# Embedding gate of a two-block transformer kernel: first weight slab tile by tile, the second tile's transposes between, embedding copies moved in ScalarE's queue

## What is computed

```python
h = h + FFN_RES_WEIGHT * swiglu(rms_norm(h, ffn2_norm[i]), ffn2_w_in[i], ffn2_w_out[i])
ple_gate = jax.nn.sigmoid(rms_norm(h, ple_norm[i]) @ w_ple_gate[i])
h = h + ple_gate * (p[i] @ w_ple_proj[i])
```

## Time and profile before

| | us |
|---|---|
| median of 3 runs | 1374.62 (1373.52 to 1375.25) |
| profiled execution | 1375.29 |
| its span, first to last instruction | 1373.5 |
| mean granted TensorE clock | 0.981 of full speed |

### The profile page before, as it was taken

The page is one execution under the profiler, slowest core; times in us unless marked ns, Lnnn a source line. Parts: engine busy times, 40 slices in busy tenths (PEclk is TensorE's granted clock), DMA queues, the critical chain, the costliest instruction groups (busy, mean ns, idle before and its releaser), DMA issues.

```text
span 1373.5 us, 23083 instructions
## 1 busy us (share of the span) xinstructions
PE 1330.2 (97%) x9022; PEld 1212.8 (88%) x9022; DVE 942.6 (69%) x1369; ACT 766.1 (56%) x1150; POOL 203.3 (15%) x165
## 2 busy tenths in 40 slices
PE   9999999999999999999999999989999999999997
PEld 8999989888998999989998889989998777777775
DVE  6555575486566555566688775765765799999996
ACT  5333346565545333355554677325734677777774
POOL 1222220030001222220301322410001000202020
PEclk9999999999999999999999999989998999999999
DMA  9655544522345555534443344215455599999991
GB/s 315 212 185 188 185 143 155 187 93 93 131 153 175 191 185 186 178 127 154 162 159 127 123 139 136 93 62 181 138 172 184 205 403 363 342 368 335 372 330 43
DMA packets 73943, 263.44 MB, mean 192 GB/s; under 512 B 8320, under 2 KB 9600, under 8 KB 73728
## 3 DMA queue, kind: packets, MB, share of 16 engines
q1 hardware_dynamic: 72864, 260.39, 55.2%
q10 hardware_dynamic: 992, 1.86, 0.4%
HBM read 261.17 MB, written 1.05 MB: 191 GB/s over the span
## 4 chain that ended last, share of the span: by engine, by line
PE 70%; DVE 9%; ACT 4%; issue 2%; POOL 0%; DVEq 0%; ACTq 0%
PE bank L561 21%; PE bank L563 20%; PE bank L562 20%; DVE sb_wlo L518 3%; DVE sb_wlo L505 2%; PE bank L2792 1%; ACT sb_aw L1729 1%; PE bank L2771 1%; ACT sb_Uh L636 1%; DVE sb_XC L2119 1%; PE bank L653 1%; PE bank L741 1%; PE bank L2849 1%; ACT sb_XC L1700 1%; ACT sb_whi L513 0%
## 5 line engine op out<-in xcount | busy, mean ns | idle before, releaser
L505 DVE TENSOR_TENSOR sb_wlo<-sb_raw,sb_whi 128x1024 fp32r<-128x1024 f32 (+2 forms) x304 | 383.4, 1306 | 168.5 <-ACT sb_whi L489 168.3
L489 ACT ACTIVATE sb_whi<-sb_raw 128x1024 fp32r<-128x1024 f32 (+3 forms) x308 | 302.0, 1031 | 227.9 <-PE bank L563 222.3
L561 PE MATMUL bank<-sb_Uh,sb_whi 128*128 128x256 f32 x1216 | 349.9, 288 | 9.7 <-ACT sb_sgh L1693 4.0
L562 PE MATMUL bank<-sb_Ul,sb_whi 128*128 128x256 f32 x1216 | 346.1, 285 | 0.0
L563 PE MATMUL bank<-sb_Uh,sb_wlo 128*128 128x256 f32 x1216 | 346.0, 285 | 0.0
L561 PEld LDWEIGHTS bank<-sb_Uh,sb_whi 128*128 128x128 f32 x1216 | 235.2, 193 | 14.9 <-issue 9.4
L562 PEld LDWEIGHTS bank<-sb_Ul,sb_whi 128*128 128x128 f32 x1216 | 235.4, 194 | 1.1 <-issue 0.2
L563 PEld LDWEIGHTS bank<-sb_Uh,sb_wlo 128*128 128x128 f32 x1216 | 235.3, 194 | 0.0
L561 PE MATMUL bank<-sb_whi,sb_Uh 128*128 128x256 f32 (+3 forms) x560 | 162.3, 290 | 6.7 <-DVE sb_Ul L645 4.9
L562 PE MATMUL bank<-sb_wlo,sb_Uh 128*128 128x256 f32 (+3 forms) x560 | 160.1, 286 | 0.0
L563 PE MATMUL bank<-sb_whi,sb_Ul 128*128 128x256 f32 (+3 forms) x560 | 159.9, 286 | 0.0
(11 more groups left out here) (407 smaller groups left out, 2252.3 us busy)
## 6 DMA issues: line engine op xcount, KB each, us to landing
sb_raw<-in_slabs SPq DMA_DIRECT2D x162, 512.0 KB, 4.5
sb_raw<-in_ffn_in SPq DMA_DIRECT2D x88, 512.0 KB, 4.6
sb_raw<-in_moe_in SPq DMA_DIRECT2D x50, 512.0 KB, 5.6
sb_raw<-in_ffn_out SPq DMA_DIRECT2D x44, 512.0 KB, 3.9
sb_raw<-in_moe_out SPq DMA_DIRECT2D x26, 512.0 KB, 6.0
sb_deep_free<-in_moe_in SPq DMA_DIRECT2D x16, 512.0 KB, 5.7
sb_deep_uh<-in_moe_in SPq DMA_DIRECT2D x16, 512.0 KB, 5.2
sb_deep_ul<-in_moe_in SPq DMA_DIRECT2D x16, 512.0 KB, 6.0
```

The costliest lines, as they stand in the source:

```text
L489: nc.scalar.activation(whi[:, i % NSLOT, c], raw[:, i % NSLOT, c], ACT.Copy).then_inc(S("hi_done"), 1)
L505: nc.vector.tensor_tensor(wlo[:, i % NSLOT, c], raw[:, i % NSLOT, c], whi[:, i % NSLOT, c].bitcast(F32), ALU.subtract).then_inc(S("lo_done ...
L561: pe.matmul(o, lh, rh, start=start, stop=False, skip_group_check=True)
L562: pe.matmul(o, lh, rl, start=False, stop=False, skip_group_check=True)
```

## The change

In `tokens_by_pairs` the first slab can now be done tile by tile: tile 0 for all eight chunks, then a given piece of work, then tile 1. For the embedding gate that piece is the turn of tile 1, which PE did before the slab until now. The other two calls of the function stay as they were. In ACT's queue the embedding copies move behind the chunks of tile 1.

```diff
-        def tokens_by_pairs(names, banks, done, made, tile_done, in_last):
+        def tokens_by_pairs(names, banks, done, made, tile_done, in_last, next_tile=None):
...
                 if j == 0:
-                    wh, wl = wslab(s0, KD, 256)
-                    for k in range(KD):
-                        if k in (0, KD // 2):
-                            pe.wait_ge(*reach("lo_done", 2 * s0 + (2 if k else 1)))
-                        for t in range(NT):
-                            stage, base, step = made(t)
-                            pe.wait_ge(*reach(stage, base + k // step + 1))
-                            last = mm3(bank[b[t]][:, 0:256], Uh[:, k, tile_cols(t)], Ul[:, k, tile_cols(t)], wh[:, k], wl[:, k],
-                                       k == 0, k == KD - 1)
+                    if next_tile is not None:
+                        token_tile(s0, b[0], 0, Uh, Ul, KD, 256, made=made(0))
+                        next_tile()
+                        last = token_tile(s0, b[1], 1, Uh, Ul, KD, 256, made=made(1))
+                    else:
...
             act_turned("n4", 0, "ple_norm")
+            act_turned("n4", 1, "ple_norm")
             ple_proj_out(1)
-            act_turned("n4", 1, "ple_norm")
...
             ple_proj(1)
-            for t in range(NT):
-                pe_turn("n4", t)
+            pe_turn("n4", 0)
             tokens_by_pairs([f"pgate{c}" for c in range(4)], pg_bank, "pg", lambda t: ("n4_lo", KD * t, 1), "t_x4",
-                            (6, lambda: pe_turn("n5", 0)))
+                            (6, lambda: pe_turn("n5", 0)), next_tile=lambda: pe_turn("n4", 1))
```

More of the change, by code:

```diff
@@ L678, in tokens_by_pairs @@
                 if j == 0:
-                    wh, wl = wslab(s0, KD, 256)
-                    for k in range(KD):
-                        if k in (0, KD // 2):
-                            pe.wait_ge(*reach("lo_done", 2 * s0 + (2 if k else 1)))
-                        for t in range(NT):
-                            stage, base, step = made(t)
-                            pe.wait_ge(*reach(stage, base + k // step + 1))
-                            last = mm3(bank[b[t]][:, 0:256], Uh[:, k, tile_cols(t)], Ul[:, k, tile_cols(t)], wh[:, k], wl[:, k],
-                                       k == 0, k == KD - 1)
+                    if next_tile is not None:
[3 more added lines that the diff above has]
+                    else:
+                        wh, wl = wslab(s0, KD, 256)
+                        for k in range(KD):
+                            if k in (0, KD // 2):
+                                pe.wait_ge(*reach("lo_done", 2 * s0 + (2 if k else 1)))
+                            for t in range(NT):
+                                stage, base, step = made(t)
+                                pe.wait_ge(*reach(stage, base + k // step + 1))
+                                last = mm3(bank[b[t]][:, 0:256], Uh[:, k, tile_cols(t)], Ul[:, k, tile_cols(t)], wh[:, k], wl[:, k],
+                                           k == 0, k == KD - 1)
                     last.then_inc(S("slab_used"), 1)
```

## The result

| | before | after |
|---|---|---|
| median of 20 runs, us | 1373.47 | 1375.48 |
| lowest to highest | 1370.63 to 1375.25 | 1370.15 to 1377.82 |
| profiled execution, span | 1375.29, 1373.5 | 1373.34, 1371.5 |

The ratio after to before is 1.0017, with a 95% interval of 1.0009 to 1.0025: slower by 2.3 us, 1.2 to 3.4. The ratio itself is inside the 0.2% that was called no change; the interval ends above it.

What follows compares the result with a forecast made beforehand. PE, busy 97% of the span, bounds the kernel, so time is won only where it stands still or runs at low clock. -0.53 + 1.46 = +0.93 us on the 1374.62 median gives 1375.55, stated as 1375.5; range 1373.0 to 1377.4.

Steps and rivals of the forecast that it cites:

- Tile 0 and the second turn: In pgate0, PE keeps up with tile 0's corrections, then turns tile 1 at 613.08; ACT idles 1.54 us.
- T1: Time at which PE finishes tile 0 of pgate0 and tile 1's transposes start, put at 613.08 us.
- ACT's way to the split: On ACT, tile 1's chunks (3.24 us) and copies (0.96) precede pgate1's split, at 617.92, 1.53 us later than before.
- The stall: PE waits 2.34 us for pgate1's first half, about 2.2 as counted; pgate1 starts 0.53 us sooner than before.
- The clock: PE's clock falls to 1.2 GHz behind the new idle before pgate1, costing 1.46 us; bounds 0 and +1.46.
- case B: Stall moved to before pgate1, clock stays at 2.4 GHz: -0.53 us, 1374.1; chance 0.28.
- case A: The forecast: stall moved to before pgate1, clock falls, +0.93 us, range 1374.6 to 1376.5; chance 0.58.
- The sum: Whole kernel: -0.53 us at pgate1's start plus 1.46 for the low clock gives +0.93 us.
- C: Gain comes whole, pgate1's first half ready by 617.96: -2.87 us, 1371.75; chance 0.05.
- D: The chunk-paced part of pgate0 itself runs at the low clock: +2.7 us, 1377.35 or above; chance 0.09.

Runs made afterwards that it cites:

- after_2: The changed kernel timed again with no edit; 1.0016 (1.0004 to 1.0029) of the kernel before.
- before_fill: The kernel before with 14 matmuls on zeros added on PE behind the two turns; 0.9996 of the kernel before.
- early_half: The changed kernel with pgate1's first half split between the two tiles' chunks, second half behind tile 1, then copies; 0.9985 and 0.9987 of the kernel before.
- copies_only: The kernel before with only the embedding copies moved behind tile 1's chunks in ACT's queue, PE's order kept; 0.9990 of the kernel before.

## Why the prediction came out

The forecast was 1375.5 and the median after is 1375.48. That it is so close is luck, two errors that cancel: the 1374.62 it started from was the median of three runs and stood at 1373.47 after twenty, and against +0.93 us the runs show +2.3, 1.2 to 3.4. The direction was right, the new stall and its cause came out as worked out, and so did the price of a fall; the size of the whole was too small.

- **Tile 0 and the second turn.** T1 was put 613.08 - 608.20 = 4.88 us behind the first turn; it is 611.18 - 606.30 = 4.88. ACT's idle of 1.54 us: 1.54.
- **ACT's way to the split.** Forecast 9.72 us behind the first turn, measured 10.00. Tile 1's chunks took 615.34 - 611.82 = 3.52 us up to the copies, not 3.24: there is one wait of 0.35 us ahead of the last chunk that tile 0 doesn't have. A like one of 0.50 us stood in tile 1 of the kernel before, and the chunks from 647.41 that I went by have none. What causes it was not tried.
- **The stall.** Forecast 2.34 us between streams, 2.2 as counted; measured 2.17. The slower chunks of tile 1 put off the end of pgate0 and the split alike, so the stall kept its size while all of it came 0.27 us later: pgate1 was to start 0.53 us sooner and starts 0.26 sooner.
- **The clock.** Forecast 1.46 us when it falls; measured 1.49. In the first profile it held, case B, in the next three it fell, case A. The Trainium skill (TensorE: Matmul & The Clock Gate, section What's actually happening) says that the monitor's window is free-running and that its effect therefore varies between runs; the four profiles agree, with one kernel, one idle of 2.17 us, and both outcomes. The rows that the forecast read it from were single outcomes too. In the thirteen profiles the idle of 1.82 us at 273 was followed by a fall in 8, that of 2.05 at 415 in 12, that of 1.68 at 385 in none. The prediction also left out one of nearly that last length in the kernel before, behind which the clock did fall, at 202.1 us; it fell there in 3 of the 13. The length of the idle alone doesn't decide. Timeline of PE, before:

```profile
200.58 1.06 PE L653 MATMUL bank<-sb_C,sb_xn 128*128 128x128 f32 x8 [1.67 <-issue]
```

- **The sum.** With these terms, -0.26 + 1.49 + 0.09, the stage is 19.91 - 18.59 = 1.32 us longer where the clock falls in both kernels. The 0.09 was not in the forecast; the first three matmuls behind the new idle hand over after 0.46 us (618.67 to 619.13) and not 0.36. The terms that were mis-sized are this and the start of pgate1, by 0.27. The four profiles after average 19.54 us, 0.95 more than the one before. That is just short of the measured 1.2 to 3.4, and inside the interval of `after_2` (0.5 to 4.0). If the clock had held in the stage before (17.11 us, as in `before_fill`), it would be 2.43. I know that state from only one profile of the kernel before, and the clock elsewhere scatters the runs by several microseconds (around 200 and 272 us, and behind 902). So the mechanism is shown in the stage; how much of the 2.3 us it makes, between 0.95 and all, stays open.
- **The cases.** C, the whole gain, needed pgate1's first half early; `early_half` supplied just that and the stage shortened by 2.48 of the 2.87 us. D, a low clock in the paced part, was not seen in any profile of the changed kernel.

## What to carry to other kernels

When one engine's stall is taken away, look at what the other engines did under its cover: here a split with 2.12 us of slack became the next stall, and moving 0.96 us of copies out of a wait that the change itself had just made on ScalarE was the wrong direction. Put the work that is needed next into such a wait first, in pieces that fit. And where the clock may or may not fall behind an idle, compare the stage in several profiles, counted from an instruction close by, and not the whole kernel in one.

## What the runs showed of the hardware

An idle of TensorE of 2.17 us was followed by a stretch at 1.2 GHz in three executions and not in a fourth, at a price of 1.49 us; one of 2.19 us in `copies_only` was not followed by one in its profile, and none of 1.20 us or less in this stage was. Outside of the stage, in code that is the same in all thirteen profiles, a fall (counted when it began between 1.1 us before the idle's end and 2 us behind it) came with an idle of 1.67 to 1.71 us at 200 in 3 of 13, with 1.68 at 385 in none, with 1.82 at 273 in 8, with 2.05 at 415 in 12, with 2.95 at 750 in 12 and with 2.62 at 900 in 11. Eight matmuls on zeros in the idle of 2.17 us went with 2.4 GHz behind it in the one profile taken, and with runs 3.0 us shorter than those of the changed kernel, at the same start of pgate1; 14 of them in the idle of 3.16 us went with a stage 1.48 us shorter.
